# Mixture-of-experts stage of a hybrid decoder step: blocks of 32 token rows in four column tiles instead of 64 in two

## What is computed

```python
def _hier_moe(x, lp):
    ...
    g_w, g_idx = lax.top_k(p_group, 1)
    ...
    e_w, e_idx = lax.top_k(jax.nn.softmax(logit_e, axis=-1), TOP_K_INNER)
    gates = g_w * e_w / jnp.sum(e_w, axis=-1, keepdims=True)
    eid = (g_idx * EXPERTS_PER_GROUP + e_idx).reshape(-1)
    ...
    def expert_block(args):
        xe, e = args
        return (jax.nn.silu(xe @ w1[e]) * (xe @ w3[e])) @ w2[e]
```

## Time and profile before

| | us |
|---|---|
| median of three runs | 3474.33 |
| fastest, slowest of the three | 3473.26, 3489.41 |
| time of the profiled execution | 3482.01 |
| its span (first to last instruction) | 3480.2 |
| PE, DVE, ACT, POOL busy | 3171.5, 1315.8, 1014.9, 331.2 |

### The profile page before, as it was taken

How to read it: one execution, slowest core, us unless ns; L and a number is a source line. 1 busy time by engine, 2 the same in 40 slices (tenths; PEclk the granted TensorE clock), 3 DMA queues, 4 the chain that set the end, 5 groups by cost and what they waited for, 6 DMA issues and landing times. The chain is left out here.

```text
span 3480.2 us, 75176 instructions
## 1 busy us (share of the span) xinstructions
PE 3171.5 (91%) x31053; PEld 2171.7 (62%) x31054; DVE 1315.8 (38%) x3229; ACT 1014.9 (29%) x2151; POOL 331.2 (10%) x348
## 2 busy tenths in 40 slices
PE   6999999999969888887999979996999999999990
PEld 4667666677738888876877755554555555555550
DVE  3454444554214433433755446664111111111117
ACT  3334433344212222223644453341111111111112
POOL 0000000000010000001433200001110101010104
PEclk9999999999779999998999889997999999999995
DMA  6121111211362332235766546422778686687658
GB/s 207 62 70 64 51 58 51 70 57 49 60 157 100 119 118 89 106 124 174 225 181 183 150 137 213 156 95 95 280 242 285 239 285 234 217 283 242 234 192 303
DMA packets 299222, 544.44 MB, mean 156 GB/s; under 512 B 98338, under 2 KB 122658, under 8 KB 292308
## 3 DMA queue, kind: packets, MB, share of 16 engines
q1 hardware_dynamic: 253180, 401.42, 34.7%
q10 hardware_dynamic: 25000, 66.13, 6.0%
q0 software_dynamic: 20784, 73.15, 5.7%
HBM read 400.66 MB, written 139.98 MB: 155 GB/s over the span
## 5 line engine op out<-in xcount | busy, mean ns | idle before, releaser
L294 PE MATMUL proj_main_ps<-proj_xt,proj_w 128*128 128x257 f32 (+1 forms) x1728 | 391.5, 382 | 0.0
L294 PEld LDWEIGHTS proj_main_ps<-proj_xt,proj_w 128*128 128x128 f32 x1728 | 329.0, 204 | 41.8
L2516 PE MATMUL moe_y_ps<-moe_w,moe_ht 128*64 128x512 f32 x1312 | 301.2, 601 | 3.1 <-ACT moe_ht L2555 3.1
L317 PE MATMUL proj_main_ps<-proj_w,proj_xt 128*128 128x512 f32 (+1 forms) x560 | 248.6, 597 | 0.0
L2264 PE MATMUL out_proj_ps<-out_w,out_ct 128*128 128x512 f32 x544 | 241.5, 597 | 6.2 <-DMA out_w<-in_w_out_dram 6.2
L2566 ACT ACTIVATE moe_sg<-moe_gate 128x256 f32<-128x256 f32 x82 | 31.5, 384 | 535.7 <-PE moe_gate L2500 535.7
L2516 PEld LDWEIGHTS moe_y_ps<-moe_w,moe_ht 128*64 128x64 f32 x1312 | 87.3, 137 | 158.7 <-issue 155.4
L1148 DVE COPY_PREDICATED rwkv_t<-rwkv_cons,rwkv_level_ps 128x512 f32<-128x512 uint32 (+1 forms) x168 | 109.2, 659 | 188.6 <-PE rwkv_level_ps L866 188.4
L317 PEld LDWEIGHTS proj_main_ps<-proj_w,proj_xt 128*128 128x128 f32 (+1 forms) x560 | 102.8, 185 | 124.4 <-issue 122.8
L2264 PEld LDWEIGHTS out_proj_ps<-out_w,out_ct 128*128 128x128 f32 x544 | 101.5, 192 | 122.0 <-issue 121.2
L2602 DVE COPY moe_y<-moe_y_ps 128x512 f32<-128x512 f32 x82 | 56.7, 692 | 313.8 <-PE moe_y_ps L2516 313.8
(11 more groups left out here) (339 smaller groups left out, 5463.3 us busy)
## 6 DMA issues: line engine op xcount, KB each, us to landing
moe_w<-in_expert_w_dram SPq DMA_DIRECT2D x64, 2048.0 KB, 9.7
y_rows<-rwkv_zero POOLq DMA_DIRECT2D x65, 512.0 KB, 4.8
kept_first_gate<-in_expert_w_dram SPq DMA_DIRECT2D x16, 2048.0 KB, 9.8
kept_first_up<-in_expert_w_dram SPq DMA_DIRECT2D x16, 2048.0 KB, 15.1
y_rows<-moe_y ACTq DMA_DIRECT2D x164, 128.0 KB, 6.1
ft_p<-proj_uf SPq DMA_DIRECT2D x32, 642.0 KB, 3.3
rwkv_feat<-ft_p SPq DMA_DIRECT2D x16, 1284.0 KB, 7.1
att_s_k<-in_cache_att_k_dram ACTq DMA_DIRECT2D x14, 1024.0 KB, 6.0
```

Source lines behind the costliest of these rows:

```text
L294: last = mm(out[:, 0:w + 1], W[:, k, kind * C + m * P:kind * C + (m + 1) * P], XT[n % 2][:, k, 0:w + 1], start=(k == 0), stop=(k == KT - 1))
L317: last = mm(o, x, W[:, k, j * C:(j + 1) * C], start=(k == 0), stop=(k == KT - 1))
L2516: last = mm(py[j * HB:(j + 1) * HB, :], HT[:, c, r * HB:(r + 1) * HB], W2[s][:, k, j * 512:(j + 1) * 512], start=(k == 0), stop=(k == FE / ...
```

## The change

Blocks have 32 rows (`HB`, `SHIFT`), gathered as quarter rows of 256. PE uses four column tiles of 32 (`j` from 0 to 3), each with a quarter of the expert's columns as moving operand: 128 columns in the gate and up products, 256 in the down product. Transposes and copies halve. `Y` is stored by four DMAs instead of two. `IDX` has 197 columns instead of 132. The copy of the next index moves behind the gather, where it waits until that gather has landed. The zeroing of `y_rows` in an earlier stage (POOL's DMAs of 512 KB) shrinks from 65 to 49 DMAs, since 196 blocks of 32 rows are fewer rows than 130 of 64.

```diff
-            link(v.tensor_scalar(CI[:], CI[:], 6, None, ALU.arith_shift_right))
+            link(v.tensor_scalar(CI[:], CI[:], SHIFT, None, ALU.arith_shift_right))
...
-HB = 64
-NBMAX = 129
+HB = 32
+NQ4 = P // HB
+SHIFT = 5
+NBMAX = 194
...
-                    for j in range(2):
+                    for j in range(NQ4):
                         last = nc.tensor.matmul(table[j * HB:(j + 1) * HB, 0:NBC], HOTP[:, n, :], HOTB[:, n, :], start=(n == 0), stop=(n == NA - 1), skip_group_check=True)
...
-    HF = FE // 2
+    HF, DQ = FE // NQ4, D // NQ4
+    KQ = DQ // P
...
-        X, XT = sb("x", [P, D // 2]), sb("xt", [P, KT // 2, P])
-        SG, HD, HT, Y = sb("sg", [P, HF]), sb("hd", [P, HF]), sb("ht", [P, 2, P]), sb("y", [P, D // 2])
+        X, XT = sb("x", [P, DQ]), sb("xt", [P, KQ, P])
+        SG, HD, HT, Y = sb("sg", [P, HF]), sb("hd", [P, HF]), sb("ht", [P, P]), sb("y", [P, DQ])
...
-                for k in range(KT // 2):
+                for k in range(KQ):
                     last = nc.tensor.transpose(px[:, k * P:(k + 1) * P], X[:, k * P:(k + 1) * P], ident[:])
...
-                    q, r = k % (KT // 2), k // (KT // 2)
-                    for j in range(2):
+                    q, r = k % KQ, k // KQ
+                    for j in range(NQ4):
                         last = mm(bank[j * HB:(j + 1) * HB, 0:HF], XT[:, q, r * HB:(r + 1) * HB], W[:, k, j * HF:(j + 1) * HF],
...
-                for c in range(2):
-                    last = nc.tensor.transpose(ph[:, c * P:(c + 1) * P], HD[:, c * P:(c + 1) * P], ident[:])
+                last = nc.tensor.transpose(ph[:, 0:P], HD[:], ident[:])
...
-                    c, r = k % 2, k // 2
-                    for j in range(2):
-                        last = mm(py[j * HB:(j + 1) * HB, :], HT[:, c, r * HB:(r + 1) * HB], W2[s][:, k, j * 512:(j + 1) * 512],
+                    for j in range(NQ4):
+                        last = mm(py[j * HB:(j + 1) * HB, 0:DQ], HT[:, k * HB:(k + 1) * HB], W2[s][:, k, j * DQ:(j + 1) * DQ],
...
-                for j in range(2):
-                    nc.scalar.dma_start(y_rows[bass.ds(b * HB - HB, HB), j * 512:(j + 1) * 512], Y[j * HB:(j + 1) * HB, :]).then_inc(y_st, 16)
+                for j in range(NQ4):
+                    nc.scalar.dma_start(y_rows[bass.ds(b * HB - HB, HB), j * DQ:(j + 1) * DQ], Y[j * HB:(j + 1) * HB, :]).then_inc(y_st, 16)
...
-            half_rows = hn.rearrange("n (a d) -> (n a) d", a=2)
+            quarter_rows = hn.rearrange("n (a d) -> (n a) d", a=NQ4)
+
+            def index(b):
+                if not start_of_all(b):
+                    g.wait_ge(x_ld, 16 * b)
+                nc.gpsimd.tensor_copy(IX[:], IDX[:, bass.ds(b, 1)]).then_inc(ix_ready, 1)
 
             def load_x(b):
-                nc.gpsimd.tensor_copy(IX[:], IDX[:, bass.ds(b, 1)]).then_inc(ix_ready, 1)
                 g.wait_ge(ix_ready, b + 1)
                 g.sem_inc(go, 1)
-                g.indirect_dma_start(X[:], None, half_rows, bass.IndirectOffsetOnAxis(ap=IX[:], axis=0)).then_inc(x_ld, 16)
+                g.indirect_dma_start(X[:], None, quarter_rows, bass.IndirectOffsetOnAxis(ap=IX[:], axis=0)).then_inc(x_ld, 16)
 
             def step(b, s, i, first):
                 g.wait_ge(x_turned, b + 2)
                 load_x(b + 2)
-
+                index(b + 3)
...
-                v.wait_ge(y_st, 32 * b)
-                v.tensor_copy(Y[:], py[:]).then_inc(y_ev, 1)
+                v.wait_ge(y_st, 64 * b)
+                v.tensor_copy(Y[:], py[:, 0:DQ]).then_inc(y_ev, 1)
```

More of the change, by code:

```diff
@@ L2316 @@
 FE = 512
-HB = 64
-NBMAX = 129
+HB = 32
+NQ4 = P // HB
+SHIFT = 5
+NBMAX = 194
 def moe_blocks(tokens):
     assert NBMAX >= 2 * tokens // HB + 2 * E
-    return NBMAX + 1
+    return NBMAX + 2
 NBC = NBMAX + 3
@@ L2334, in dispatch_consts @@
     token = np.where(token < prompt + sample, token, 0)
-    half = np.repeat(np.arange(2), HB)[:, None]
+    quarter = np.repeat(np.arange(NQ4), HB)[:, None]
     row = lambda n: np.broadcast_to(np.arange(n), (P, n))
-    return np.ascontiguousarray(np.concatenate([row(HB), row(NBC), 2 * np.repeat(token, 2, 1), half], 1).astype(np.float32))
+    return np.ascontiguousarray(np.concatenate([row(HB), row(NBC), NQ4 * np.repeat(token, 2, 1), quarter], 1).astype(np.float32))
 def dispatch(nc, consts, SLOT, IDX, w1, w3, W1, W3, loaded):
@@ L2349, in dispatch @@
         places, numbers = cn[:, 0:HB], cn[:, HB:HB + NBC]
-        token2, half = cn[:, HB + NBC:HB + NBC + NA], cn[:, HB + NBC + NA:]
+        token4, quarter = cn[:, HB + NBC:HB + NBC + NA], cn[:, HB + NBC + NA:]
         bi = sb("block_int", [P, NA], I32)
@@ L2374, in _ @@
             v.tensor_copy(slot[:], flat)
-            v.tensor_scalar(bi[:], flat, 6, None, ALU.arith_shift_right).then_inc(step, 1)
+            v.tensor_scalar(bi[:], flat, SHIFT, None, ALU.arith_shift_right).then_inc(step, 1)
             v.wait_ge(step, 1)
@@ L2385, in _ @@
             v.wait_ge(listed, 1)
-            v.tensor_scalar(rows[:], table[:, 0:NBC], half, None, ALU.add).then_inc(step, 1)
+            v.tensor_scalar(rows[:], table[:, 0:NBC], quarter, None, ALU.add).then_inc(step, 1)
             v.wait_ge(step, slots_split + 1)
@@ L2395, in _ @@
                 g.wait_ge(at_place, i + 1)
-                nc.gpsimd.tensor_tensor(HOTP[:, k[0]:k[1], :], HOTP[:, k[0]:k[1], :], each(token2, k, HB), ALU.mult).then_inc(at_token, 1)
+                nc.gpsimd.tensor_tensor(HOTP[:, k[0]:k[1], :], HOTP[:, k[0]:k[1], :], each(token4, k, HB), ALU.mult).then_inc(at_token, 1)
         @blk.tensor
@@ L2464, in _ @@
             sp.dma_start(ident[:], ident_in).then_inc(id_in, 16)
-            sp.sem_inc(y_st, 32)
+            sp.sem_inc(y_st, 64)
             down(0, 0)
@@ L2478, in _ @@
             end = sp.value_load(BT[0:1, E + 1:E + 2], min_val=2 * E, max_val=NBMAX)
-            sp.wait_ge(y_st, 32 * end + 32)
+            sp.wait_ge(y_st, 64 * end + 64)
             sp.sem_inc(ended, 1)
@@ L2550, in xt @@
                     a.wait_ge(h3, b)
-                nc.scalar.copy(XT[:].rearrange("p k t -> p (k t)"), px[:]).then_inc(xt_ready, 1)
+                nc.scalar.copy(XT[:].rearrange("p k t -> p (k t)"), px[:, 0:DQ]).then_inc(xt_ready, 1)
             def ht_before(b):
                 a.wait_ge(h_turned, b)
-                nc.scalar.copy(HT[:].rearrange("p k t -> p (k t)"), ph[:, 0:2 * P]).then_inc(ht_ready, 1)
+                nc.scalar.copy(HT[:], ph[:, 0:P]).then_inc(ht_ready, 1)
             def store_before(b):
                 a.wait_ge(y_ev, b + 1)
-                for j in range(2):
-                    nc.scalar.dma_start(y_rows[bass.ds(b * HB - HB, HB), j * 512:(j + 1) * 512], Y[j * HB:(j + 1) * HB, :]).then_inc(y_st, 16)
+                for j in range(NQ4):
+                    nc.scalar.dma_start(y_rows[bass.ds(b * HB - HB, HB), j * DQ:(j + 1) * DQ], Y[j * HB:(j + 1) * HB, :]).then_inc(y_st, 16)
             def step(b, s, i, first):
@@ L2590, in step @@
                 load_x(b + 2)
+                index(b + 3)
+            index(0)
             load_x(0)
+            index(1)
             g.wait_ge(x_turned, 1)
             load_x(1)
+            index(2)
             over_experts(g, step)
```

## The result

The changed kernel takes **3595.9 us** (median of 4 runs, 3585.3 to 3598.4); the kernel before, run beside it, 3473.8. The ratio is 1.034, 95% interval 1.030 to 1.039. The forecast was 3594 us, range 3495 to 3680, slower with 0.86.

The account below looks back on a forecast made before the run. PE alone bounds the experts' stage before; afterwards the gather loop decides under the weights. PE's work -43, gathers with open code between experts +155, clock +8: +120, a median of 3594 us, range 3495 to 3680.

Parts of the forecast that it names:

- PE's work: Experts' stage: 147 blocks at 6.18 us of PE make 908 us, so PE's work falls by 43 us.
- rival 2: PE's products: four column tiles do not run together, +707, 4181 us; chance 0.04.
- Code between experts: PE's code at 31 passages: 2.1 us on average, 0.9 hidden by the down product, 1.2 open each, 37 us.
- Gathers: Gather loop of X: under the weights it outlasts PE's block; 155 us with PE's open code between experts included.
- The second gather: Gather at the passage, behind POOL's code: loop of 8.75 us against 6.18 of PE, 2.57 of waiting per expert.
- The first: First gather of an expert under the weights: 7.4 us against 6.18 + 1.2, nothing beyond PE's own 1.2.
- The third: Third gather of an expert, still under the weights: loop of 7.4 us, costing 1.22 per expert.
- Rival 1: Gather loop: smaller gathers slip through the weights, landing in 4.9 us or less; 3468 or 3431 us; chance 0.14.
- Clock: PE after the second gather's wait: lower clock, mostly absorbed by the third loop's slack; +8 us, bounds 0 and 53.
- Rival 4: PE's clock stays down longer, one more stretch of 3.4 us per expert: +53, 3640 to 3690; chance 0.09.
- Stores: Store loop of Y: 7.65 to 8.55 us under the weights, staying behind the gathers, so nothing is counted.
- rival 3: Store loop of Y decides at 8.55 us under the weights, PE waiting before the down product: +124, 3598; chance 0.11.

Follow-up runs that it names:

- no_weights: The changed kernel without weight transfers from the third expert on (output of those experts wrong): 3451.5 us, ratio 0.993 to 1.000 to the kernel before.
- experiment 1: The changed kernel with the weight transfers left out from the third expert on, all gathers, stores and products kept: 3451.5 us.
- experiments 5 and 6: 5: changed kernel plus a second buffer between gather and transpositions, 3514.1 us; 6: one store for four, on that kernel and another, 3641.7 and 3620.1 us.
- two_x: The changed kernel with a second buffer, copied by GpSimd, between the gather and the transpositions: 3514.1 us, ratio 1.009 to 1.016 to the kernel before.
- small_packets: The changed kernel with weights fetched in packets of 1 KB in place of 2 and 4 KB: 3581.8 us, ratio 1.023 to 1.036 to the kernel before.

## Why the prediction was right, point by point

Worked out in terms of the stage, forecast +120, measured +126.2:

- **PE's work, -43.** PE busy in the stage without traffic is 913.3 against 956.8: **-43.5**. The block is 6.12 us (6.18 forecast), gate 1.86, up 1.89, y 1.75, transposes 0.37 and 0.26. Four column tiles of 128 partitions run together: rival 2 is out. The longer loops cost nothing to fetch: the loop over two experts has 1304 instructions where it had 688, but PE's code at a passage lasts 1.6 or 2.1 us as before, and from 2540 to 3490 no DMA queue fetches instructions; the trace has only these (packets, MB, share):

```profile
q1 hardware_dynamic: 70416, 169.87, 48.6%
q10 hardware_dynamic: 25037, 17.12, 6.4%
q0 software_dynamic: 6240, 17.05, 5.4%
```

  That agrees with the Trainium skill ("Runtime: NRT & Kernel Launch", Instruction fetch mechanics) as far as its 128 KiB for PE go, and speaks against a stall at each branch.
- **Code between experts, 1.2 x 31 = 37.** Measured 0.69 us of idle time each, **22.7** with two short waits for the input copy; by the turns it is 0.90 (7.02 us at the first turn of no_weights against 6.12), 28 us. The code is as long as forecast: 1.6 and 2.1 us in turn, and 0.3 until the next product, 2.16 on average. The lead was mis-sized. At every passage the code starts 0.48 us into the y product, 1.27 ahead of the moment at which the next product could start, where I had 0.9; 2.16 - 1.27 is the 0.9 that lies open. At the passage above (y product from 2914.90):

```profile
L2446 PEldq ALU_OP  x1: 36/36/36, 2915.4 to 2915.4; - x1
...
L2444 PEldq SEQ_ASSERT  x1: 18/18/18, 2917.0 to 2917.0; - x1
```

- **Gathers, 155 - 37 = 118.** Measured **111.7**, but the parts differ. The second gather, 8.75 with 2.57 of waiting: 8.63 and 2.47, the step on which most hung. The first, "nothing beyond PE's own 1.2": 1.1 on top of the code, since it lands after 6.72, not 6.0, and the code hides less. The third, 1.22: nothing, since it met only the end of the weights (landing 3.24). They flow for 19 us, not 20.7, as the weights' queue and the GB/s in slices of 0.49 us from 2916.4 show, and the gather of 2932.89 is nearly behind them. One miss of +1.1 and one of -1.22 cancel, which is luck. Rival 1 is out: it needed landings below 4.9 us under the weights, and they were 6.7 and 6.1.

```profile
GB/s 100 301 209 318 364 376 401 364 263 339 393 395 395 399 410 403 414 401 414 401 405 389 393 389 410 414 385 420 383 420 403 420 403 435 418 401 234 251 59 8
...
q1 hardware_dynamic: 2589, 6.25, 85.5%
```

- **Clock, +8, bounds 0 and 53.** Measured **+34.4** of busy time, some 31 of it the clock (experiment 1). This is the term that was most mis-sized. I had let the third block's slack take most of the loss up; but that slack was in the gather's loop, and in the third block PE, not the gather, decides (it had landed 2.5 us early), so each stretch at the lower level costs its full 1.7 us of work. Rival 4, a further stretch per expert, didn't come: 20 in all, for 31 passages.
- **Stores, nothing.** VectorE waited 3.2 us for one, PE 3.6 before a y product: rival 3 is out, and experiments 5 and 6 show what it looks like when it isn't.
- **Sum.** -43.5 + 22.7 + 111.7 + 34.4 + 5.4 of two single waits (3.6 and 1.8) - 4.6 that PE had been idle before = +126.1. The signs, the places and the order of the waits were as forecast; the closeness of 3594 to 3595.9 owes something to luck: a clock term some 26 too small, with the ends of products in it, against a code term 14 and gathers 6 too large.
- **Checks named ahead.** y to gate 1.75; per expert 8.16, 8.63, 7.16, 6.12 where I had 7.4, 8.75, 7.4, 6.2; waits for `moe_x` 111.7 ("near 120"); issue before the gate product 21.7 ("some 40").

What the forecast didn't see is that the moved copy was about half of the loss, 57 to 70 us in the stage: it named the 2.57 us of waiting, and gave the clock behind them 0.3 us.

## What to carry to other kernels

Halving a block's work halves the time in which its transfers must come round, and a transfer's latency under load doesn't halve: before shrinking blocks, set each single-buffered loop, at its loaded latency, against the new block. When an instruction that waits is moved in an engine's queue, look at what stands behind it, the loop's own register code included; one place in the queue was worth 70 us of the stage. And price a wait by what follows it too: here the lower clock followed most of the waits of 2 us and more, and added some 31 us to 112 of waiting.

## What was new of the hardware

- A gather of 128 rows landed after 2.76 us alone and 5.5 to 6.7 under a stream of weights at some 340 GB/s, whether the weights' packets had 2 and 4 KB or 1 KB, and half the bytes took 0.6 us off a gather alone, but nothing that shows off the first under the weights (6.7 against 6.6, means over 31 experts).
- A store whose pattern has an outermost dimension of four ran on four of the 16 DMA engines (share 0.25), and landed after 9.3 us under the weights; four stores of the same bytes landed in some 6.8 in two_x, counted from the first issue.
- With gathers that went out 0.26 us later the gate products beside them were slower, 11.3 us of busy PE over 147 blocks, with no weights flowing. The cause is open.
- After 19 of 32 waits of 2 us and more the granted clock fell to its lower level for 3.4 us, after 2 of 64 shorter ones. In small_packets it was 10 of 92 waits between 0.3 and 2 us: the length of the wait alone doesn't decide it.
